# Two-pass output stage of a hybrid decoder layer: mix and norm of all tiles, then the gate of two tiles at once by seven half products

## What is computed

```python
z = einsum('btd,dc->btc', x, w_in)                     # one input projection
attn, o_hg = ...                                       # window attention; gated linear recurrence
mix = einsum('btc,cd->btd', concat([attn, o_hg]), w_out)
h = layernorm(DN_ALPHA * x + mix, ln_g, ln_b)
gate = sigmoid(einsum('btd,de->bte', h, w_ple_gate))   # 1024 x 1024
y = h + gate * einsum('btp,pd->btd', p, w_ple_proj)    # 256 x 1024
```

## Time and profile before

| | us |
|---|---|
| median of 3 runs (2610.28 to 2618.58) | 2614.02 |
| profiled execution: its own time | 2612.2 |
| its span, first to last instruction | 2610.2 |
| PE busy | 2550.8 (98% of the span) |
| DVE busy | 1670.2 (64%) |
| ACT busy | 1055.2 (40%) |
| POOL busy | 906.4 (35%) |

### The profile page before, as it was taken

One profiled execution on the slowest core, in us unless ns is written; L12 is line 12 of the kernel. 1 busy time (PEld: TensorE's weight loads), 2 busy tenths in 40 slices (PEclk: granted clock), 3 DMA queues, 4 the chain that ended last, 5 costly groups with the idle time before them and its releaser, 6 DMA issues. The chain is left out here.

```text
span 2610.2 us, 55103 instructions
## 1 busy us (share of the span) xinstructions
PE 2550.8 (98%) x20946; PEld 2091.5 (80%) x20946; DVE 1670.2 (64%) x3130; ACT 1055.2 (40%) x2396; POOL 906.4 (35%) x899
## 2 busy tenths in 40 slices
PE   7999989999999999999999999899999999999999
PEld 6788767888888778888878888678888887888887
DVE  5667777777677655555556767776777775455453
ACT  4444455555555411111234444455555553111111
POOL 2222215555655612122112222165555655122121
PEclk9999999999999999999999999999999999999999
DMA  5344541011110845545632544510111018333332
GB/s 177 118 153 149 176 170 52 26 46 46 42 38 32 341 100 121 115 103 119 186 110 97 192 149 137 192 34 30 42 53 39 30 57 335 87 85 94 94 84 61
DMA packets 314498, 281.59 MB, mean 108 GB/s; under 512 B 206400, under 2 KB 259648, under 8 KB 312256
## 3 DMA queue, kind: packets, MB, share of 16 engines
q1 hardware_dynamic: 252976, 271.88, 32.7%
q10 hardware_dynamic: 61360, 7.44, 1.9%
HBM read 176.80 MB, written 89.65 MB: 102 GB/s over the span
## 5 line engine op out<-in xcount | busy, mean ns | idle before, releaser
L123 PE MATMUL r_Z<-w_rec_high,w_rec_xh 128*128 128x512 f32 x960 | 391.5, 408 | 1.8 <-DVE r_kT L1644 0.9
L123 PE MATMUL r_Z<-w_rec_high,w_rec_xl 128*128 128x512 f32 x960 | 375.7, 391 | 0.0
L123 PE MATMUL r_Z<-w_rec_low,w_rec_xh 128*128 128x512 f32 x960 | 374.5, 390 | 0.0
L123 PE MATMUL a_Z<-w_attn_high,w_attn_xh 128*128 128x512 f32 (+1 forms) x816 | 303.9, 372 | 12.6 <-DVE w_attn_low L229 12.6
L123 PE MATMUL a_Z<-w_attn_low,w_attn_xh 128*128 128x512 f32 (+1 forms) x816 | 292.1, 358 | 0.0
L123 PE MATMUL a_Z<-w_attn_high,w_attn_xl 128*128 128x512 f32 (+1 forms) x816 | 291.2, 357 | 0.0
L1524 ACT ACTIVATE r_E<-r_E 128x512 f32<-128x512 f32 x230 | 145.4, 632 | 294.9 <-DVE r_E L1681 292.5
L1415 POOL TENSOR_TENSOR r_qE<-r_qT,r_E 128x256 f32<-128x256 f32 x230 | 184.0, 800 | 199.5 <-ACT r_E L1524 135.4
L123 PEld LDWEIGHTS r_Z<-w_rec_high,w_rec_xl 128*128 128x128 f32 x960 | 180.1, 188 | 39.8
L123 PEld LDWEIGHTS r_Z<-w_rec_high,w_rec_xh 128*128 128x128 f32 x960 | 180.3, 188 | 38.9 <-issue 3.6
L123 PEld LDWEIGHTS r_Z<-w_rec_low,w_rec_xh 128*128 128x128 f32 x960 | 180.7, 188 | 33.0
(11 more groups left out here) (313 smaller groups left out, 5456.9 us busy)
## 6 DMA issues: line engine op xcount, KB each, us to landing
dram_w_parts<-w_attn_part_high SPq DMA_DIRECT2D x36, 512.0 KB, 2.7
dram_w_parts<-w_attn_part_low SPq DMA_DIRECT2D x36, 512.0 KB, 4.0
w_out_high<-dram_w_parts SPq DMA_DIRECT2D x36, 512.0 KB, 8.0
w_out_low<-dram_w_parts SPq DMA_DIRECT2D x36, 512.0 KB, 10.8
dram_y_all<-o_hb SPq DMA_DIRECT2D x34, 512.0 KB, 3.0
w_attn_xraw<-dram_xT SPq DMA_DIRECT2D x33, 512.0 KB, 4.7
w_rec_whole<-dram_w_in SPq DMA_DIRECT2D x16, 1024.0 KB, 12.6
o_mraw<-dram_mixT SPq DMA_DIRECT2D x32, 512.0 KB, 4.7
```

What stands on the lines that cost most here:

```text
L123: mm = pe.matmul(out, a[:, c, :], b[:, c, :], start=(first and c == chunks[0] and a is xh and b is wh), stop=(last and c == chunks[-1] and ...
```

## The change

1. The output stage is made in two passes. Pass one does mix, norm and turn of all 17 tiles; h goes to DRAM twice, as rows and transposed (four DMAs of 128-byte pieces a tile, in both layers). Mix uses two PSUM tiles in turn, and PE transposes nothing.
2. Pass two takes tiles 1 and 2, 3 and 4, ... as pairs, and tile 0 alone. The gate of a pair is a product of 2x2 blocks (128 tokens x 512 by 512 x 512) by Strassen's method: seven half products of 12 matmuls, where the plain product has eight. POOL makes five sums of h blocks and seven low parts a pair, ACT seven high parts, one copy of a bank and the tanh by halves, DVE six adds of 128x512. Strassen's two-bank results are partly accumulated in PSUM (`onto`). ple and embed of both tiles follow.
3. The seven blocks (sums) of w_gate, "slots", are formed in attention: 24 parts instead of 18, twelve of them a layer summed by POOL (`combine`, two operations of 128x512 each). The part buffer is double. Parts are stored to `g_parts`, 1 MB for each half of a slot.
4. Loads are placed anew. Five slots are loaded in pass one; slots 4 and 6, which lie where w_out's low parts lay, and w_proj after it. The masks of layer 1's attention, its weights, two chunks of the recurrence's weights, the recurrence's first x and the norm's rows are loaded later than before.

The core of it:

```diff
 (attention, SP)
             sp.wait_ge(*S["x_split"].at(NT))
+            sp.wait_ge(*S["part_st"].at(32 * PARTS))
             lead.load_x(sp, 0)
...
-            following.load(sp, dram, layer, 4, following.chunks)
+            following.load(sp, dram, layer, 4, 6)
             store_mix(PAIRS - 1, 1)
+            sp.wait_ge(*S["pv_done"].at(NT))
+            following.load(sp, dram, layer, 6, following.chunks)
 (attention, SP, layer 1)
             load_x(1, 1)
+            if layer > 0:
+                sp.wait_ge(*prior["yT_st0"].at(64 * (PAIRS + 1)))
+                sp.wait_ge(*prior["yT_st1"].at(64 * PAIRS))
+                load_masks(*masks[1:])
 (attention, POOL, in the loop over pairs, c = 4 * (j - 1))
                 split_low(j + 1, 0)
+                combine(c - 1)
                 rope_sum(j, 1)
+                combine(c)
                 root(j, 0)
                 split_low(j + 1, 1)
+                combine(c + 1)
                 rope_sum(j + 1, 0)
+                combine(c + 2)
 (output, SP)
+            for n in range(NT):
+                k = n % 2
+                if 0 < n < NT - 1:
+                    load_row(n + 1)
+                if n + 3 < NT:
+                    load_m(n + 3)
+                if n in (2, 4, 6, 8):
+                    w.load_slot(sp, dram, layer, n // 2 - 1)
...
+                store_h(n, k)
...
+            sp.wait_ge(*S["low_read"].at(1))
+            w.load_slot(sp, dram, layer, 4)
+            w.load_slot(sp, dram, layer, 6)
+            sp.wait_ge(*S["summed"].at(NT))
+            load_p(2, 1, 0)
+            load_p(1, 0, 0)
+            w.load_proj(sp, dram, layer)
...
+            def store_h(n, k):
+                sp.wait_ge(*S["h_done"].at(n + 1))
+                sp.dma_start(dram["h_rows"][layer, n], hb[k][:, :]).then_inc(h_st[k].sem, 16)
+                sp.wait_ge(*S["turned"].at(n + 1))
+                for to, of in turned_to(hT[k], dram["hT"][layer, n]):
+                    sp.dma_start(to, of).then_inc(hT_st[k].sem, 16)
 (output, SP, last pair of layer 0)
+                    for product, first, last in ((1, 0, 3), (2, 3, 6), (3, 6, KC)):
+                        sp.wait_ge(*S["product"].at(ahead_of(q, 7, 7) + product))
+                        lead.load(sp, first, last)
 (output, ACT)
+            for k in range(6):
+                high(k, 0)
+            high(6, 0)
+            act.wait_ge(*hT_st[1].at(64 * PAIRS))
+            high_ps(0)
+
+            third(0)
+            tanh_b1(0)
 (output, DVE, last pair of layer 0)
+                lead.remainder(dve, 3, KC)
+            embeds(q)
 (output, PE)
+            def unit(q):
+                for k in range(7):
+                    if first:
+                        if k in (0, 4):
+                            w.slots_arrived(pe, layer, k // 4)
...
+                    elif k >= 4:
+                        pe.wait_ge(*S["recombined"].at(6 * q + k - 3))
+                    product(k, k, k >= 4).then_inc(S["product"].sem, 1)
...
+                ple(1, at, at)
+                ple(0, at + 1, at)
+            with pe.Fori(1, PAIRS) as j:
+                mix(2 * j, 0)
+                mix(2 * j + 1, 1)
+            mix_last(NT - 1, 0)
+            unit(0)
```

More of the change, by code:

```diff
@@ L186, in of @@
-    def of(self, c):
[L188 to L205, removed]
-                self.load_part(sp, dram, layer, c, part)
-    def arrived_parts(self, pe, layer, c):
-        pe.wait_ge(self.arrived[c], self.counts(c, layer))
+        self.chunks, self.arrived, self.counts, self.rows = chunks, arrived, counts, rows
@@ L493, in attention_phase @@
         own, before = slice(P, 2 * P), slice(0, P)
-        part, part_high, part_low = (weights.beside[n] for n in ("part", "part_high", "part_low"))
+        part = [weights.beside[n] for n in ("part0", "part1")]
+        part_high, part_low = (weights.beside[n] for n in ("part_high", "part_low"))
+        part_in = S["part_in0"], S["part_in1"]
+        upper, lower = (weights.beside[n][:, :, :].rearrange("p b d -> p (b d)") for n in ("kc", "vc"))
         @block.sync
@@ L2056, in _, with ahead_of, output_phase @@
             transpose_u(n)
-def output_phase(nc, block, layer, C, dram, S, weights, lead, first_part, prior):
+def ahead_of(q, pair, single):
+    return pair * q + (0 if isinstance(q, int) and q == 0 else single)
+def output_phase(nc, block, layer, C, dram, S, space, lead, first_part, prior):
     more = layer < DEPTH - 1
@@ new lines, in high_ps, with third, sigmoid @@
+            def high_ps(q):
+                for k in (1, 0):
+                    high_p(k, ahead_of(q, 2, 1) + 2, ahead_of(q, 2, 1))
+            def third(q):
+                act.wait_ge(*S["product"].at(ahead_of(q, 7, 7) + 3))
+                wait(act, S["recombined"], 6 * q)
+                act.activation(c3[:, :], C12, ACT.Copy).then_inc(S["c3_done"].sem, 1)
+            def sigmoid(k, half, of):
+                act.activation(th[k][:, halves[half]], of, ACT.Tanh, scale=0.5).then_inc(S["tanh_done"].sem, 1)
@@ L2423, in _ @@
-            mm.then_inc(S["gate_ps"].sem, 1)
-            turn_h(1, 1)
-            for c in range(2 * KC, weights.chunks):
-                weights.arrived_parts(pe, layer, c)
-            ple(0)
-            gate(1)
-            ple(1)
-            with pe.Fori(1, PAIRS - 1) as j:
-                step(2 * j, 0)
-                step(2 * j + 1, 1)
-            n = NT - 1
-            step(n - 2, 0)
-            mix(n, 0, 0)
-            mix(n, 1, 0)
-            gate(n - 1)
-            turn_h(n, 0)
@@ new lines, in product, with ple @@
+            def product(k, of, onto):
+                wh, wl = w.slots[k]
+                for c in range(KC // 2):
+                    for a, b in ((bh[of], wh), (bh[of], wl), (bl[of], wh)):
+                        mm = pe.matmul(bank[k], a[:, c, :], b[:, c, :], start=(not onto and c == 0 and a is bh[of] and b is wh),
+                                       stop=(c == KC // 2 - 1 and a is bl[of]), skip_group_check=True)
+                return mm
+            def ple(k, at, ahead):
+                pe.wait_ge(*S["p_split"].at(at + 1))
+                wait(pe, S["blend"], ahead)
+                for half in halves:
+                    mm = split_products(pe, PL[k][:, half], ph[k], pl[k], w.proj[0][:, :, half], w.proj[1][:, :, half],
+                                        range(PC), True, True)
+                mm.then_inc(S["ple_ps"].sem, 1)
```

961 lines of the change are left out of this document (563 added, 398 removed).

## The result

| | before | after |
|---|---|---|
| median | 2613.82 us (4 runs, 2610.28 to 2618.58) | 2662.93 us (4 runs, 2659.46 to 2665.74) |
| ratio to before | | 1.0186, 95% interval 1.0165 to 1.0207 |
| profiled execution, span | 2610.2 us | 2662.3 us |

A forecast was written before the change was run, and what follows sets the result against it. PE was taken as the bound: the steady output stage costs what its matmuls cost. Against the profiled 2612.2 us, -48.8 + 3 + 38 + 4 + 8 + 2 + 9 = +15.2 gave 2627 us, range 2600 to 2648.

The forecast's parts named there:

- Matmuls, -48.8: Output stages: fewer gate matmuls (-43.5) and no turns of h by PE (-5.3) save 48.8 us together.
- Pass one, +3: Output stage, pass one: 11.2 us of queue work a tile against PE's 10.88, mostly hidden by reserve; +1.5 us a layer.
- the queue sets the pace: Rival, chance 0.15: DMA queue paces pass one; at 12.5 us a tile, 8 us a layer more, 2643 us.
- Slots 4 and 6, +38: Output stage: PE waits 19 us a layer before product 4; loads out at t+14, t being the end of mix_last.
- w_proj ... adds nothing: Output stage, after the slots: w_proj needs 5 us more but is wanted 13 us later, so no added cost.
- The clock, +4: Behind the wait for slots 4 and 6: a lowered PE clock loses 2 us a layer, +4 (0 to 8).
- Attention to recurrence, +8: Before the recurrence: x loaded later, ACT's exponentials 4.9 us late, then DVE and PE; 4 us a layer.
- Attention's loop, +2: Attention: extra parts cost 0; four of POOL's twelve combines make DVE wait beside the small maxima; +2 us (0 to 12).
- The rival with 0.08: Rival, chance 0.08: POOL's combines block attention by holding DVE's chain to PE; a layer loses 14 us more, 2653 us.
- The boundary, +9: Between layers: weights issued later, rope starts 2 to 4 us late, masks ready late and PE waits; +9 us (4 to 14).

The follow-up runs named there:

- e4: Changed kernel with the transposed h stored in pieces of 1 KB instead of 128 bytes, readers permuting: 2639.44 us, ratio to before 1.0102.
- e1: Changed kernel with the loads of slots 4 and 6 issued ahead of the stores of h of tile 15: 2658.47 us, ratio to before 1.0181.
- e2: Changed kernel with ACT's copy of C12 (third) ahead of the two splits of p: 2663.51 us, ratio to before 1.0190.
- e3: Changed kernel with the edits of e1 and e2 together: 2660.24 us, ratio to before 1.0177.
- e8: e7 with layer 0's transposed y also in 1 KB pieces, layer 1's readers permuting, and the recurrence's second lead tile loaded in four parts: 2611.51 us, ratio 0.9996.
- e9: e8 with layer 1's first x and attention weights loaded ahead of a y store, and the masks ahead of the window copies: 2608.94 us, ratio 0.9983.
- e7: Changed kernel with e4's pieces, e1's slot order, and ACT's copy of C12 ahead of the splits of block 6 and p: 2620.33 us, ratio 1.0034.

## Why the prediction was right or wrong

**Matmuls, -48.8: right.** 24.48 us a pair, 240 PE instructions fewer.

**Pass one, +3, with the reserve to hide the queue: the step that failed first.** I priced the transposed store at 4.96 us, the time that SP was held in the earlier trace rows, on a queue with room. In pass one, four such stores hold SP for 6.8 and 8.4 us in turn, and a tile takes 12.0 us, where I had counted 11.2 of queue work. The rival "the queue sets the pace" had named 12.5 and 8 us a layer; the waits are 7.6 and 5.6 us besides that of the start, and the clock's dips. I gave it 0.15 although my own count stood at 11.2 against 10.88. e4 shows that it is the pieces.

**Slots 4 and 6, +38: right in size (19.3 + 19.7 = 38.9), half right in cause.** The chain that I wrote down (slots, p, ACT's copy of C12, first sum) is the one in the trace, but I had not seen that slots and stores share one backlog, so that whichever goes last is late, nor that block 6 hangs on tile 16's stores. Acting on my account alone, as e1, e2 and e3 do, brings nothing that can be told from the runs' spread. The size is in part luck. With t at 1093.3 (1123.48 less the wait and four products), the loads went out at t+12.2 and not t+14, because SP's stores held it for 3.0 us there and not 5.0; but from the first issue to landing the slots took 14.5 us (1105.78 to 1120.29 in e2) where I had 12.5. The two errors cancel.

**The term that was missing: waits behind the wait.** 4.4 and 2.5 us before product 4 of the second pair. I wrote "w_proj ... adds nothing" and stopped there, but h and p of the pairs that follow are loaded in the same backlog, behind stores on which SP is held. POOL's sums for the third pair wait for its h, ACT's first splits of these sums wait for POOL, and the copy for the second pair's first sum stands behind the splits:

```profile
1164.01 6.20 POOL L2296 TENSOR_TENSOR o_tmp<-o_raw 128x512 f32<-128x512 f32 x5 [1.95 <-DMA o_raw<-dram_hT]
...
1166.42 0.58 ACT L2400 ACTIVATE o_c<-o_MX 128x512 f32<-128x512 f32 x1
```

**The clock, +4: low, it is about 10.** In the two output stages 51 matmuls of 128x512 (28 and 23) start 0.43 us apart, and none before the change: 51 x 0.20 us. Layer 0 alone has two such stretches behind a wait of product 4, 1124 to 1128 us and behind 1168, and one at the boundary; the waits in pass one bring more.

**Attention to recurrence, +8: wrong, it is nothing (-0.9 and -0.1 over the whole recurrence).** ACT did wait for the x split, 6.6 us in layer 1:

```profile
1670.42 1.34 ACT L248 ACTIVATE w_rec_xh<-w_rec_raw 128x256 fp32r<-128x256 f32 x4 [6.60 <-DMA w_rec_raw<-dram_xT]
1671.66 0.35 ACT L785 ACTIVATE w_attn_probs<-a_SC,a_nmax 128x128 f32<-128x128 f32 x1
...
1668.25 0.16 DVE L918 TENSOR_TENSOR a_sinkd<-a_nmax,a_nsink 128x4 f32<-128x4 f32 x1
...
1680.83 0.65 PE L1191 MATMUL a_T<-w_attn_pT,a_v 128*64 128x256 f32 x4 [1.17 <-DVE w_attn_pT L967]
```

But the exponentials could not have begun before DVE's row at 1668.25, as the wait of 3.67 us in the earlier trace rows already says; they start 3.2 us late instead of 4.9, and of that PE feels 0.7 at the next value product (1.17 where 0.45 stood). I had taken a delay on ACT as a delay on PE without counting the projections that PE has in between.

**Attention's loop, +2: wrong, 9.7 and 3.9.** The rival with 0.08 had the mechanism, but not its size: it named 14 us a layer, 28 in all, and 13.6 in all are measured. I had put eight of POOL's combinations beside operations that read PSUM, and no wait of PE stands behind those. The four beside the small maxima, the place that I named as open, hold one or two operations a step for 1.2 to 1.3 us, and the delay passes through the exponentials to u and pT, where PE had no reserve.

**The boundary, +9: 13.9 to the decode tile's u.** The mask's wait and the embeds behind the remainders are as described; the wait for the first x (another 3.3 us, counted to the output stage in the table) and the lower clock behind these waits (0.67 from 1354 to 1364 us) are not in my sum. e8 shows that the small pieces of y's stores are part of it.

The two output stages balance: PE's waits of 0.25 us or more grew by 62.7 us and the lower clock took 10, against 48.8 of matmuls saved, so 24 of the 25.6 us that the table gives for them.

In sum, against 15.2 predicted and 52.1 measured in the spans: attention gives 11.6 more, the two output stages 26.1, the boundary with its wait for x 8.2, the way to the recurrence and through it 9.0 less.

## What to carry to other kernels

When a change routes data through DRAM, count packets and not only bytes, and price a store in the queue as full as it will be. When several inputs of one operation are late, taking away one of them shows nothing: change all of them together, then take them away one at a time. A stream of an in-order engine that is held by a full queue delays everything written behind it, so what is needed first goes first, ahead of stores that nobody waits for. Look for the waiter first, though: e3's and e9's stores had one, the engine that writes the same buffer next.

## What the runs showed of the hardware

- With the same 363.11 MB on the queue in the whole run, the DMA engines were busy for 0.92 of pass one with 4096 pieces of 128 bytes a tile, and for 0.76 with 512 of 1 KB, while PE got further (740 matmuls for 699 in the same 172 us).
- Issuing is no fixed cost, and small pieces make it dear: four stores of 128-byte pieces (128 KB each) held SP for 3.0 to 9.8 us in pass one of the changed kernel and for 13.6 us behind 4.2 MB of slots (e3); in pieces of 1 KB they held it for 1.8 to 2.2 us in pass one and for 1.75 behind the same slots (e7).
- A DVE operation of 0.16 us with two inputs of 4 elements a partition in SBUF took 1.2 to 1.3 us where it met a POOL operation of 1.3 us (eight of 68 in layer 0); halving POOL's operations gives back half of the mean.
- DVE's transpose in blocks of 32x32 of a 128x1024 tile took 1.25 us as well when input and output were permuted views (34 in e4, 34 in the changed kernel).
